# Expert loop of a two-block layer stack: GpSimd makes the low part of every fourth weight piece, and the loads wait for pieces to be used

## The chip, the cores and the metric

The kernel runs on one core of a Trainium2 chip. Its time is the device time of one execution in microseconds (us); lower is better. The engines are TensorE (PE; its weight loads are PEld), VectorE (DVE), ScalarE (ACT), GpSimd (POOL) and SyncE (SP), whose queue issues most of the loads from the chip's memory (HBM).

## What is computed

Two transformer-like blocks run one after the other on 256 tokens of width 1024, each with two layers. The change touches only the mixture of experts of the first block's second layer:

```python
def moe_ffn(h, router_w, w1, w3, w2):
    logits = (h @ router_w).astype(jnp.float32)
    top_vals, top_idx = lax.top_k(logits, TOP_K)            # 2 of 8 experts
    top_w = jax.nn.softmax(top_vals, axis=-1)
    gate = jnp.sum(jax.nn.one_hot(top_idx, N_EXPERTS, dtype=jnp.float32) * top_w[..., None], axis=-2)
    out = jnp.zeros_like(h)
    for e in range(N_EXPERTS):
        out = out + gate[..., e:e + 1].astype(h.dtype) * swiglu(h, w1[e], w3[e], w2[e])
    return out
```

`swiglu` is `(silu(h @ w1) * (h @ w3)) @ w2`, with `w1` and `w3` of 1024x2816 and `w2` of 2816x1024, all float32.

## The kernel before

**Passes.** After the router the kernel knows which tokens go to which expert. A pass is one expert with up to 128 of its tokens; the number of passes is read at run time, and the same loop body (`Fori`) runs on every engine. This input makes 8 passes.

**Steps and pieces.** Within a pass the hidden width of 2816 is cut into 11 chunks of 256, done in 12 steps, c = 0 to 11. Step c multiplies the tokens by chunk c of `w1` and `w3` (pieces q = 0 to 3, in steps 0 to 10) and the hidden values of chunk c-1 by its part of `w2` (pieces q = 4 and 5, in steps 1 to 11). A piece is 128 partitions by 1024 float32. A pass has 66 pieces (`ALL_PIECES`), numbered n in the order of PE's use: step 0 has n = 0 to 3, and step c has n = 6c-2+q.

**Split products.** To keep float32 precision each piece is split in two: ACT copies it to the rounded type fp32r (`w_hi`), and the low part is the piece minus `w_hi` (`w_lo`). PE then makes three products of 512 columns for each half of the piece: tokens' high part by `w_hi` (line 824), tokens' low part by `w_hi` (825), high part by `w_lo` (826), so 6 matmuls a piece. `w_hi` and `w_lo` have four places each (`NPIECE`), and piece n lies in place n % 4.

**Who waits for whom.** In the expert loop ACT (line 1551) makes `w_hi` of piece n when PE has used piece n-4 (semaphore `e_used`); DVE makes `w_lo` (its operation is recorded at the helper's line 2182) when `e_hi_ready` has counted piece n; PE waits for `e_split`, which DVE's low part raises. In other stages of the program GpSimd makes low parts too (line 700), by the same subtraction in the same shape.

**Other work of a step.** When q = 3 is used, ACT makes silu (L1569, output `xs`), DVE multiplies (L2346, `u_z`; one input in PSUM, the accumulators' memory), and PE turns the result by two transposes (L1106) at the start of the next step. ACT copies those out (`fhT_hi`, L1564), and DVE makes their low part (`fhT_lo`, L2182, one input in PSUM). DVE's order within a step is fhT_lo, low parts of q = 3, 4, 5 and of q = 0 of the next step, u_z, low parts of q = 1 and 2 of the next step. ACT's order is the same with high parts.

**Loads.** Weights land in three slots (`ring` 0 and 1, `third_gu`, each with a part of `down_w`); step c uses slot c % 3. SP issues the loads of step c (three of 1 MB; two in step 0, one in step 11) when all pieces of step c-3 are split (`e_split`, line 641). At the first step of the first pass the counts that open the loop come from two operations: DVE's copy of `slot_no` (line 2247) adds `ALL_PIECES` to `e_split`, and the fourth of PE's opening matmuls on `pb` (line 1084) adds `NPIECE` to `e_used`.

**Edges of a pass.** PE gathers the tokens of the next pass (L1093) and scatters the results (L1128); ACT and DVE copy the results out (L1571, L2353). Then ACT and DVE make the parts of pieces 0 to 2 and of the tokens (`hT_hi`, L1557, and `xg_lo`), and in the first steps DVE makes the selection tables (L2331 to L2335, L2297, L2298).

Of the kernel before, what the change touches and what calls it, by code (L numbers as in the profile page):

```python
# [15 lines left out]
F32 = mybir.dt.float32  # L16
# [3 lines left out]
ALU = mybir.AluOpType  # L20
# [14 lines left out]
NF = FF // FC  # L35
# [16 lines left out]
NSLOT = 3  # L52
# [183 lines left out]
def build(nc, a, out):  # L236
# [6 lines left out]
    with ctx:  # L243
# [176 lines left out]
            "sel_ready", "gather_mm", "xg_ready", "selT_ready", "scatter_mm", "ys_ready"))  # L420
        e_arrived = [sem(f"e_arrived{n}") for n in range(NSLOT)]
        e_silu, e_h, e_ht_mm, e_ht_hi, e_ht = (sem(s) for s in ("e_silu", "e_h", "e_ht_mm", "e_ht_hi", "e_ht"))
        zero_ready, moe_mm, sel_step = sem("zero_ready"), sem("moe_mm"), sem("sel_step")

        def step_loads(c):
# [181 lines left out]
        def expert_piece(c, q):  # L607
# [2 lines left out]
                return gu_slot(c % NSLOT)[:, q * PIECE:(q + 1) * PIECE]  # L610
            return down_w[:, c % NSLOT, (q - GU_PIECES) * PIECE:(q - GU_PIECES + 1) * PIECE]

        def slot_split(c):

            return pieces(c + 1) if c < NF else ALL_PIECES
# [17 lines left out]
        def expert_weights(sp):  # L633

            n_pass = passes(sp)
            with sp.Fori(0, n_pass) as t:
                e = sp.value_load(table[0:1, bass.ds(t, 1)], min_val=0, max_val=NE - 1)
                for c in range(NF + 1):
                    s = c % NSLOT

                    sp.wait_ge(e_split, t * ALL_PIECES + (ALL_PIECES + slot_split(c - NSLOT) if c >= NSLOT else slot_split(NF + 1 - NSLOT + c)))
                    srcs = []
                    if c < NF:
                        for view, w_ in ((gate_view, a["moe_w1"]), (up_view, a["moe_w3"])):
                            srcs.append((view, w_[0, bass.ds(e, 1), :, c * FC:(c + 1) * FC].rearrange("o (k p) n -> p (o k) n", p=P)))
                    if c:
                        srcs.append((down_view, a["moe_w2"][0, bass.ds(e, 1), (c - 1) * FC:c * FC, :].rearrange("o (k p) n -> p (o k) n", p=P)))
                    for view, src in srcs:
                        sp.dma_start(view(s, src), src).then_inc(e_arrived[s], 16)
            sp.wait_ge(e_split, n_pass * ALL_PIECES + ALL_PIECES)  # L650

# [41 lines left out]
        def _(pool):  # L695
# [47 lines left out]
            load_gain(5, a["g_pre_mix_2"][0])  # L743
            pool.wait_ge(gla_put, 10)
            pool.dma_start(cst2, cdram2[:, :]).then_inc(cst2_in, 16)
            for l in range(2):
                L, n = 2 + l, 5 + 4 * l
                if l:
                    load_gain(n, a["g_pre_mix_2"][l])
                low_parts(MIX[L], MIX[L] + 4)  # L750
                load_gain(n + 1, a["g_post_mix_2"][l])

                pool.wait_ge(merged_ready, 2 + l)
                for lo, w, name in ((0, MW, "g_cq_2"), (MW, P, "g_ckv_2"), (MW + P, MW, "g_sgu_v_2")):
                    pool.dma_start(ygain[:, lo:lo + w], a[name][l].partition_broadcast(P)).then_inc(ygain_in, 16)
                for aa in range(2):
                    for b_ in range(2):
                        pool.dma_start(pool_w[64 * b_:64 * b_ + 64, aa, :], a["pool_w_2"][l, 2 * aa + b_]).then_inc(pool_in_sem, 16)
                pool.wait_ge(filled, BK[L].filled(("turn", 3)))
                pool.dma_start(sgu_w, a["sgu_w_2"][l].rearrange("g i j -> i g j")).then_inc(sgu_in, 16)  # L760
                low_parts(MIX[L] + 4, MIX[L] + 40)
                pool.wait_ge(merged_ready, L + 1)
                load_gain(n + 2, a["g_pre_ffn_2"][l])
                load_gain(n + 3, a["g_post_ffn_2"][l])
                low_parts(MIX[L] + 40, MIX[L] + 44)
# [4 lines left out]
        def _(pe):  # L770
# [291 lines left out]
            def experts():  # L1062
# [20 lines left out]
                for n in range(4):  # L1083
                    ins = mm(pb[n][:], ident, scratch[:], start=True, stop=False, skip_group_check=True)
                    if n == 2:
                        ins.then_inc(scatter_mm, 1)
                    if n == 3:
                        ins.then_inc(e_used, NPIECE)

                def gather():  # L1090
                    for k in range(KD):
# [8 lines left out]
                with pe.Fori(0, n_pass) as t:  # L1100
                    pe.wait_ge(xg_ready, t + 1)
                    for n, (c, q) in enumerate(PIECE_LIST):
# [4 lines left out]
                            ins.then_inc(e_ht_mm, 1)  # L1107
                        if q == GU_PIECES:
                            pe.wait_ge(e_ht, t * NF + c)
                        pe.wait_ge(e_split, t * ALL_PIECES + ALL_PIECES + n + 1)  # L1110
                        if q < GU_PIECES:
                            for kk in range(2):
                                k = 2 * q + kk
# [230 lines left out]
        def _(act):  # L1344
# [195 lines left out]
            def experts():  # L1540
# [3 lines left out]
                with act.Fori(0, n_pass) as t:  # L1544
                    def high_parts(lo, hi):
                        for n in range(lo, hi):
                            c, q = PIECE_LIST[n]
                            if n == pieces(c):
                                act.wait_ge(e_arrived[c % NSLOT], e_landed(t, c))
                            act.wait_ge(e_used, t * ALL_PIECES + place_free(n) + NPIECE)  # L1550
                            f(w_hi[:, n % NPIECE], expert_piece(c, q), ACT.Copy).then_inc(e_hi_ready, 1)  # L1551

                    high_parts(0, 3)
# [5 lines left out]
                    for c in range(NF + 1):  # L1559
                        if c:  # L1560
                            high_parts(at, min(pieces(c) + 3, ALL_PIECES))
                            at = min(pieces(c) + 3, ALL_PIECES)
                            act.wait_ge(e_ht_mm, t * NF + c)
                            f(fhT_hi[:, :, 0:P], mb[3][:, 0:2 * P].rearrange("p (k s) -> p k s", k=2), ACT.Copy).then_inc(e_ht_hi, 1)  # L1564
                        if c < NF:
                            high_parts(at, pieces(c + 1) + 1)
                            at = pieces(c + 1) + 1
                            act.wait_ge(e_used, t * ALL_PIECES + pieces(c) + GU_PIECES + NPIECE)
                            f(fsg[:, 0, :], mb[2][:, 0:FC], ACT.Silu).then_inc(e_silu, 1)  # L1569
                    act.wait_ge(e_used, t * ALL_PIECES + ALL_PIECES + NPIECE)  # L1570
# [134 lines left out]
        def _(v):  # L1705
# [536 lines left out]
            def route():  # L2242
# [1 line left out]

                v.wait_ge(logits_mm, 1)
                link(cp(logit.rearrange("p t e -> p (t e)"), mb[0][:, 0:2 * NE]))
                cp(slot_no, const("iotap")).then_inc(e_split, ALL_PIECES)
                v.wait_ge(e_split, ALL_PIECES)
                rk = const("rank8").unsqueeze(1).to_broadcast([P, T, NE])
                wide = lambda col: col.unsqueeze(2).to_broadcast([P, T, NE])  # L2250
                for src, top, one in ((logit, m1, one1), (tmp16, m2, one2)):
# [51 lines left out]
            def experts():  # L2303
# [3 lines left out]
                with v.Fori(0, n_pass) as t:  # L2307
# [8 lines left out]
                    def low_parts(lo, hi):  # L2316
                        for m in range(lo, hi):
                            c, q = PIECE_LIST[m]
                            v.wait_ge(e_hi_ready, t * ALL_PIECES + m + 1)
                            low(w_lo[:, m % NPIECE], expert_piece(c, q), w_hi[:, m % NPIECE]).then_inc(e_split, 1)  # L2320

# [14 lines left out]
                    for c in range(NF + 1):  # L2336
# [10 lines left out]
                        if c == 0:  # L2347
# [1 line left out]
                            qv = quad[:, 0:2].rearrange("p q t -> p (q t)")  # L2349
                            step(ts(qv, qv, -float(P), None, ALU.add))  # L2350
                            select_places(step)
                    v.wait_ge(e_used, t * ALL_PIECES + ALL_PIECES + NPIECE)
                    cp(ys[:, 512:1024], mb[1][:]).then_inc(ys_ready, 1)  # L2353
                assert n[0] == 7, n[0]
                v.wait_ge(moe_mm, 1)
# [54 lines left out]
```

## Time and profile before

| | |
|---|---|
| three runs | 2878.45 us median, 2877.14 to 2897.91 |
| profiled execution | 2887.1 us, of which the profiled span is 2885.3 us |
| busy in the span: PE, DVE, ACT, POOL | 90%, 56%, 46%, 17% |
| low parts by POOL, whole program | 184, mean 2431 ns |
| low parts by DVE from `ring`, whole program | 352, mean 1223 ns |
| granted TensorE clock over the span | 0.94 of full speed |

Times in the rows below are microseconds from the start of the span. In a row of the timeline the first number is the start, the second the duration; "x2" merges two instructions of the same kind, whose durations then read as one stretch. Matmuls overlap: each shows some 0.4 us, but the next one of the same kind starts 0.23 us later. A bracket at the end tells how long the engine idled before, and what released it. SPq is the queue of SP that issues loads.

### The profile page before, as it was taken

How to read it: one execution, taken by the hardware profiler on the slowest of the kernel's cores; microseconds unless marked ns; L12 is line 12 of the kernel's file. 1: busy time of each engine (PE TensorE's matmuls, PEld its weight loads, DVE VectorE, ACT ScalarE, POOL GpSimd, SP SyncE). 2: the span in 40 equal slices, each digit the busy share in tenths (PEclk: the TensorE clock that was granted, in tenths of full speed). 3: DMA queues.
4: the chain of work that ended last, by engine and by line, in shares of the span. 5: the costliest groups of instructions: out<-in, count | busy, mean ns of one | idle time of the engine just before them, and what ended most of it. 6: DMA issues, size and time to landing. Idle time of an engine off the chain costs nothing.

```text
span 2885.3 us, 31104 instructions
## 1 busy us (share of the span) xinstructions
PE 2600.9 (90%) x11527; PEld 2049.5 (71%) x11527; DVE 1605.2 (56%) x2251; ACT 1319.5 (46%) x1687; POOL 477.1 (17%) x248
## 2 busy tenths in 40 slices
PE   6998789989987799999999999789979978998897
PEld 5886568868865677787787787577757856775786
DVE  2545545525365398898898898732325553231654
ACT  1333144413331277777787787524324432433443
POOL 2344210003442100000000000024430002444000
PEclk9989899999898799999999999999989998989999
DMA  5423175424231499999999899443355514334550
GB/s 183 161 103 123 44 242 175 152 76 161 102 131 58 141 360 307 321 340 318 322 325 334 305 340 333 176 151 117 131 181 184 182 68 131 137 109 168 191 197 35
DMA packets 373247, 549.38 MB, mean 190 GB/s; under 512 B 20828, under 2 KB 273104, under 8 KB 373024
## 3 DMA queue, kind: packets, MB, share of 16 engines
q1 hardware_dynamic: 369072, 535.82, 54.0%
q0 software_dynamic: 3648, 9.87, 1.2%
q10 hardware_dynamic: 432, 2.37, 0.2%
q8 instruction: 66, 1.08, 0.2%
q14 instruction: 29, 0.24, 0.0%
HBM read 546.98 MB, written 1.05 MB: 190 GB/s over the span
## 4 chain that ended last, share of the span: by engine, by line
PE 63%; DVE 8%; issue 2%; DMA 2%; ACT 2%; POOL 1%; SPq 0%; ACTq 0%; DVEq 0%
PE mb L824 12%; PE mb L826 11%; PE mb L825 11%; PE pb L824 5%; PE pb L825 5%; PE pb L826 5%; PE pb L802 3%; PE pb L1152 2%; PE pb L807 2%; DMA ring<-in_w_in 1%; DVE w_lo L2182 1%; POOL w_lo L700 1%; PE mb L1172 1%; PE pb L872 1%; PE mb L1174 1%
## 5 line engine op out<-in xcount | busy, mean ns | idle before, releaser
L700 POOL TENSOR_TENSOR w_lo<-ring,w_hi 128x1024 fp32r<-128x1024 f32 x184 | 443.4, 2431 | 1875.3 <-ACT w_hi L1418 1875.1
L824 PE MATMUL mb<-w_hi,hT_hi 128*128 128x512 f32 x1232 | 500.1, 406 | 24.3 <-DVE xg_lo L2182 9.7
L2182 DVE TENSOR_TENSOR w_lo<-ring,w_hi 128x1024 fp32r<-128x1024 f32 x352 | 423.6, 1223 | 121.3 <-ACT w_hi L1418 70.6
L826 PE MATMUL mb<-w_lo,hT_hi 128*128 128x512 f32 x1232 | 486.1, 395 | 0.0
L1418 ACT ACTIVATE w_hi<-ring 128x1024 fp32r<-128x1024 f32 x280 | 285.8, 1054 | 315.8 <-DMA ring<-in_w_in 153.9
L2182 DVE TENSOR_TENSOR w_lo<-down_w,w_hi 128x1024 fp32r<-128x1024 f32 x242 | 295.2, 1223 | 93.6 <-ACT w_hi L1418 79.3
L824 PE MATMUL pb<-w_hi,hT_hi 128*128 128x512 f32 x736 | 309.0, 420 | 16.9 <-DVE low_rows L2182 7.6
L825 PE MATMUL pb<-w_hi,low_rows 128*128 128x512 f32 x736 | 299.8, 407 | 0.0
L826 PE MATMUL pb<-w_lo,hT_hi 128*128 128x512 f32 x736 | 299.1, 406 | 0.0
L824 PEld LDWEIGHTS mb<-w_hi,hT_hi 128*128 128x128 f32 x1232 | 233.1, 189 | 80.5 <-issue 22.9
L1551 ACT ACTIVATE w_hi<-ring 128x1024 fp32r<-128x1024 f32 x256 | 268.1, 1056 | 42.6 <-PE mb L826 39.3
L825 PE MATMUL mb<-w_hi,xg_lo 128*128 128x512 f32 x704 | 276.1, 392 | 0.0
L826 PEld LDWEIGHTS mb<-w_lo,hT_hi 128*128 128x128 f32 x1232 | 232.4, 189 | 56.0
L825 PE MATMUL mb<-w_hi,low_rows 128*128 128x512 f32 x528 | 206.9, 392 | 0.0
L1551 ACT ACTIVATE w_hi<-down_w 128x1024 fp32r<-128x1024 f32 x176 | 187.2, 1063 | 37.4 <-PE mb L826 32.8
L824 PEld LDWEIGHTS pb<-w_hi,hT_hi 128*128 128x128 f32 x736 | 147.2, 200 | 54.7 <-DVE low_rows L2182 8.5
L2182 DVE TENSOR_TENSOR w_lo<-third_gu,w_hi 128x1024 fp32r<-128x1024 f32 x132 | 159.4, 1222 | 41.3 <-ACT w_hi L1418 31.6
L826 PEld LDWEIGHTS pb<-w_lo,hT_hi 128*128 128x128 f32 x736 | 146.1, 198 | 32.6
L825 PEld LDWEIGHTS pb<-w_hi,low_rows 128*128 128x128 f32 x736 | 147.0, 200 | 31.1 <-issue 1.3
L825 PEld LDWEIGHTS mb<-w_hi,xg_lo 128*128 128x128 f32 x704 | 133.4, 189 | 27.2
L802 PE MATMUL pb<-hT,ring 128*128 128x256 f32 (+1 forms) x608 | 137.2, 386 | 12.5 <-DMA ring<-in_w_in 11.3
L824 PE MATMUL mb<-w_hi,fhT_hi 128*128 128x512 f32 x352 | 140.0, 398 | 8.1 <-DVE fhT_lo L2182 8.1
(412 smaller groups left out, 3755.6 us busy)
## 6 DMA issues: line engine op xcount, KB each, us to landing
ring<-in_moe_w SPq DMA_DIRECT2D x128, 1024.0 KB, 7.7
ring<-in_w_in SPq DMA_DIRECT2D x48, 2048.0 KB, 7.7
down_w<-in_moe_w SPq DMA_DIRECT2D x88, 1024.0 KB, 10.9
third_gu<-in_moe_w SPq DMA_DIRECT2D x48, 1024.0 KB, 9.1
down_w<-in_w_ffn_down SPq DMA_DIRECT2D x22, 1024.0 KB, 9.8
ring<-in_w_out SPq DMA_DIRECT2D x8, 2048.0 KB, 7.9
ring<-in_ffn_w SPq DMA_DIRECT2D x16, 1024.0 KB, 7.9
ring<-in_w_ffn_gate SPq DMA_DIRECT2D x16, 1024.0 KB, 5.2
```

The costliest lines, as they stand in the source:

```text
L700: nc.gpsimd.tensor_tensor(w_lo[:, m % NPIECE], source[m][0], w_hi[:, m % NPIECE].bitcast(F32), ALU.subtract).then_inc(pool_split, 1)
L802: ins = mm(bank[0:m, n * S:(n + 1) * S], wv[:, k, col - chunk_lo:col - chunk_lo + m], hT[:, k, :], start=k == 0, stop=k == KD - 1)
L807: ins = mm(bank[:, 0:m], hT[:, k, i * P:(i + 1) * P], wv[:, k, col - chunk_lo:col - chunk_lo + m], start=k == 0, stop=k == KD - 1)
L824: mm(o, a_hi, hi, start=start, stop=False)
L825: mm(o, a_lo, hi, start=False, stop=False)
L826: return mm(o, a_hi, lo, start=False, stop=stop)
L872: ins = mm(bank[:], yT[:, b % 2, kk, i * P:(i + 1) * P], w[:, kk, h * 512:(h + 1) * 512], start=kk == 0, stop=kk == 1)
L1152: ins = mm(bank[:], src[:, kk, i * P:(i + 1) * P], w[:, kk, h * 512:(h + 1) * 512], start=kk == 0, stop=kk == n_k - 1)
L1172: ins = mm(o, qT[:, h, it], kT[:, h, jt], start=True, stop=i != j)
L1418: f(w_hi[:, m % NPIECE], src, ACT.Copy).then_inc(w_hi_ready, 1)
L1551: f(w_hi[:, n % NPIECE], expert_piece(c, q), ACT.Copy).then_inc(e_hi_ready, 1)
L2182: return tt(dst, src, hi.bitcast(F32), ALU.subtract)
```

## The change

In the expert loop the low part of every piece with n % 4 = 3 (n = 3, 7, ..., 63: 16 of the 66 pieces) is made by GpSimd in a loop of its own, and DVE leaves it out. PE waits for the new semaphore `e_pool_split` before those pieces and for `e_split` before the others. Since one count no longer tells that all pieces of a slot are split, SP waits for `e_used` before it loads a slot, and `e_used` now starts at `ALL_PIECES`.

```diff
+        POOL_PIECES = ALL_PIECES // NPIECE
+        DVE_PIECES = ALL_PIECES - POOL_PIECES
@@ SP, expert_weights
-                    sp.wait_ge(e_split, t * ALL_PIECES + (ALL_PIECES + slot_split(c - NSLOT) if c >= NSLOT else slot_split(NF + 1 - NSLOT + c)))
+                    sp.wait_ge(e_used, t * ALL_PIECES + (ALL_PIECES + slot_split(c - NSLOT) if c >= NSLOT else slot_split(NF + 1 - NSLOT + c)))
...
-            sp.wait_ge(e_split, n_pass * ALL_PIECES + ALL_PIECES)
+            sp.wait_ge(e_used, n_pass * ALL_PIECES + ALL_PIECES)
@@ GpSimd, before the second block's layers
+            nc.gpsimd.memset(small[:, 141:142], 0.0).then_inc(e_pool_split, POOL_PIECES)
+            n_pass = passes(pool)
+            with pool.Fori(0, n_pass) as t:
+                for m in range(NPIECE - 1, ALL_PIECES, NPIECE):
+                    pool.wait_ge(e_hi_ready, t * ALL_PIECES + m + 1)
+                    nc.gpsimd.tensor_tensor(w_lo[:, m % NPIECE], expert_piece(*PIECE_LIST[m]),
+                                            w_hi[:, m % NPIECE].bitcast(F32), ALU.subtract).then_inc(e_pool_split, 1)
@@ PE, experts
                     if n == 3:
-                        ins.then_inc(e_used, NPIECE)
+                        ins.then_inc(e_used, ALL_PIECES)
...
-                        pe.wait_ge(e_split, t * ALL_PIECES + ALL_PIECES + n + 1)
+                        if n % NPIECE == NPIECE - 1:
+                            pe.wait_ge(e_pool_split, t * POOL_PIECES + POOL_PIECES + n // NPIECE + 1)
+                        else:
+                            pe.wait_ge(e_split, t * DVE_PIECES + DVE_PIECES + n + 1 - n // NPIECE)
@@ ACT: the three waits on e_used have the new start
-                            act.wait_ge(e_used, t * ALL_PIECES + place_free(n) + NPIECE)
+                            act.wait_ge(e_used, t * ALL_PIECES + place_free(n) + ALL_PIECES)
@@ DVE, low_parts
                             c, q = PIECE_LIST[m]
+                            if m % NPIECE == NPIECE - 1:
+                                continue
```

**DVE, steps 2 and 3 of a pass.** The stretch runs from the low part of q = 3 of step 2 (`third_gu`) to the low part of q = 1 of step 3 (`ring`). Before:

```order
L2182 TENSOR_TENSOR w_lo<-third_gu,w_hi 128x1024
L2319 REGISTER_ALU
L2182 TENSOR_TENSOR w_lo<-down_w,w_hi 128x1024
L2319 REGISTER_ALU
L2182 TENSOR_TENSOR w_lo<-down_w,w_hi 128x1024
L2319 REGISTER_ALU
L2182 TENSOR_TENSOR w_lo<-ring,w_hi 128x1024
L2345 REGISTER_ALU
L2346 TENSOR_TENSOR u_z<-xs,mb 128x256
L2319 REGISTER_ALU
L2182 TENSOR_TENSOR w_lo<-ring,w_hi 128x1024
```

With the change (lines are 14 to 16 higher there):

```order
L2196 TENSOR_TENSOR w_lo<-third_gu,w_hi 128x1024
L2335 REGISTER_ALU
L2196 TENSOR_TENSOR w_lo<-down_w,w_hi 128x1024
L2335 REGISTER_ALU
L2196 TENSOR_TENSOR w_lo<-ring,w_hi 128x1024
L2361 REGISTER_ALU
L2362 TENSOR_TENSOR u_z<-xs,mb 128x256
L2335 REGISTER_ALU
L2196 TENSOR_TENSOR w_lo<-ring,w_hi 128x1024
```

One of the two low parts from `down_w` (n = 15, q = 5 of step 2) is gone from DVE's order; the rest stands as it stood.

**POOL, at the place between the two blocks.** Before, the load of constants is followed by the low parts of the second block:

```order
L745 DMA cst<-shape_constants 128x1856 [waits gla_put]
L700 TENSOR_TENSOR w_lo<-ring,w_hi 128x1024 [waits w_hi_ready] x4
L728 DMA gain<-in_g_post_mix 128x1024 [waits xn_ready]
```

With the change the loop stands between them; its first rows are these:

```order
L749 DMA cst<-shape_constants 128x1856 [waits gla_put]
L750 MEMSET small 128x1
L635 TENSOR_LOAD table [waits table_ready]
L635 ISA x2
L752 UNCONDITIONAL_BRANCH
L752 ISA
L755 TENSOR_TENSOR w_lo<-ring,w_hi 128x1024 [waits e_hi_ready]
L754 REGISTER_ALU
L755 TENSOR_TENSOR w_lo<-ring,w_hi 128x1024 [waits e_hi_ready]
L754 REGISTER_ALU
L755 TENSOR_TENSOR w_lo<-third_gu,w_hi 128x1024 [waits e_hi_ready]
```

These three are n = 3, 7 and 11. The pieces that went to POOL are, by step: q = 3 of step 0, q = 3 of every odd step to 9, and q = 1 and q = 5 of every even step from 2 to 10. No other work of POOL stands within the loop.

## Rows read from the trace of the kernel before

**Rows 1.** Waits in the expert loop, 990 to 1860 us: total, times, longest.

```profile
PE mb L824 <- DVE xg_lo L2182: 9.7, 8, 3.7
PE mb L824 <- DVE fhT_lo L2182: 8.1, 8, 1.0
PE mb L1106 <- DVE u_z L2346: 7.4, 8, 0.9
...
PE mb L824 <- DVE w_lo L2182: 6.3, 8, 0.8
```

**Rows 2.** Timeline of PE, second pass, steps 1 to 3.

```profile
1123.19 0.40 PE L824 MATMUL mb<-w_hi,hT_hi 128*128 128x512 f32 x1
...
1127.38 0.38 PE L1106 MATMUL mb<-cst,u_z 128*128 128x128 f32 x2
...
1134.59 0.40 PE L824 MATMUL mb<-w_hi,fhT_hi 128*128 128x512 f32 x1
...
1135.99 0.38 PE L1106 MATMUL mb<-cst,u_z 128*128 128x128 f32 x2
```

**Rows 3.** Timeline of ACT, the same steps.

```profile
1133.39 0.39 ACT L1569 ACTIVATE xs<-mb 128x256 f32<-128x256 f32 x1 [0.34 <-PE mb L826]
...
1136.69 1.05 ACT L1551 ACTIVATE w_hi<-ring 128x1024 fp32r<-128x1024 f32 x1
...
1140.60 1.06 ACT L1551 ACTIVATE w_hi<-ring 128x1024 fp32r<-128x1024 f32 x1 [0.33 <-PE mb L826]
```

**Rows 4.** Timeline of DVE, steps 1 to 2 of that pass.

```profile
1119.02 2.35 DVE L2182 TENSOR_TENSOR w_lo<-ring,w_hi 128x1024 fp32r<-128x1024 f32 x2
...
1125.03 1.21 DVE L2182 TENSOR_TENSOR w_lo<-third_gu,w_hi 128x1024 fp32r<-128x1024 f32 x1
1126.17 0.41 DVE L2346 TENSOR_TENSOR u_z<-xs,mb 128x256 f32<-128x256 f32 x1
1126.50 2.35 DVE L2182 TENSOR_TENSOR w_lo<-third_gu,w_hi 128x1024 fp32r<-128x1024 f32 x2
```

**Rows 5.** Timelines of 203 to 206 and 244 to 246.5 us, DVE and POOL.

```profile
203.73 1.95 DVE L1950 SCALAR_TENSOR_TENSOR probs<-probs,mb 128x384 f32<-128x384 f32 x4 [8.57 <-PE mb L879]
203.74 2.41 POOL L700 TENSOR_TENSOR w_lo<-ring,w_hi 128x1024 fp32r<-128x1024 f32 x1 [2.17 <-ACT w_hi L1418]
...
244.83 2.49 POOL L700 TENSOR_TENSOR w_lo<-ring,w_hi 128x1024 fp32r<-128x1024 f32 x1 [13.29 <-ACT w_hi L1418]
244.98 3.42 DVE L1851 TENSOR_TENSOR conv<-ch_in 128x1024 f32<-128x1024 f32 x1
```

**Rows 6.** The same, 246.5 to 251 us: both of POOL's instructions in one.

```profile
244.83 5.82 POOL L700 TENSOR_TENSOR w_lo<-ring,w_hi 128x1024 fp32r<-128x1024 f32 x2 [13.29 <-ACT w_hi L1418]
```

**Rows 7.** Timeline of ACT and POOL, one piece of a stage where POOL splits.

```profile
374.77 1.06 ACT L1418 ACTIVATE w_hi<-ring 128x1024 fp32r<-128x1024 f32 x1 [1.66 <-PE pb L826]
...
375.91 2.40 POOL L700 TENSOR_TENSOR w_lo<-ring,w_hi 128x1024 fp32r<-128x1024 f32 x1 [0.32 <-ACT w_hi L1418]
```

**Rows 8.** Timeline of SP's queue, the issue of step 6's loads.

```profile
1141.69 1.00 SPq L649 DMA_DIRECT2D ring<-in_moe_w  x2
1142.87 2.03 SPq L649 DMA_DIRECT2D down_w<-in_moe_w  x1
```

**Rows 9.** Load of `down_w` issued at 1176 to 1178 us: size, landing.

```profile
down_w<-in_moe_w SPq DMA_DIRECT2D x1, 1024.0 KB, 11.3
```

**Rows 10.** Timeline around the start of the loop, 972 to 1003 us.

```profile
986.18 5.49 SPq L649 DMA_DIRECT2D ring<-in_moe_w  x4
...
990.90 3.60 PE L1084 MATMUL pb<-scratch,cst 128*128 128x512 f32 x8
...
994.60 1.28 ACT L1551 ACT_TABLE_LOAD   x1 [14.49 <-DMA ring<-in_moe_w]
```

**Rows 11.** Timeline behind the loop, 1838 to 1905 us.

```profile
1846.82 3.73 PE L1093 MATMUL mb<-gates,xn 128*128 128x128 f32 x32
...
1868.38 3.88 ACT L1418 ACTIVATE w_hi<-ring 128x1024 fp32r<-128x1024 f32 x4
```

More of the change, by code:

```diff
@@ L422, in build @@
         e_silu, e_h, e_ht_mm, e_ht_hi, e_ht = (sem(s) for s in ("e_silu", "e_h", "e_ht_mm", "e_ht_hi", "e_ht"))
+        e_pool_split = sem("e_pool_split")
         zero_ready, moe_mm, sel_step = sem("zero_ready"), sem("moe_mm"), sem("sel_step")
@@ L1567, in experts @@
                             at = pieces(c + 1) + 1
-                            act.wait_ge(e_used, t * ALL_PIECES + pieces(c) + GU_PIECES + NPIECE)
+                            act.wait_ge(e_used, t * ALL_PIECES + pieces(c) + GU_PIECES + ALL_PIECES)
                             f(fsg[:, 0, :], mb[2][:, 0:FC], ACT.Silu).then_inc(e_silu, 1)
-                    act.wait_ge(e_used, t * ALL_PIECES + ALL_PIECES + NPIECE)
+                    act.wait_ge(e_used, t * ALL_PIECES + 2 * ALL_PIECES)
                     f(ys[:, 0:512], mb[0][:], ACT.Copy).then_inc(ys_ready, 1)
@@ L2246, in route @@
                 link(cp(logit.rearrange("p t e -> p (t e)"), mb[0][:, 0:2 * NE]))
-                cp(slot_no, const("iotap")).then_inc(e_split, ALL_PIECES)
-                v.wait_ge(e_split, ALL_PIECES)
+                cp(slot_no, const("iotap")).then_inc(e_split, DVE_PIECES)
+                v.wait_ge(e_split, DVE_PIECES)
                 rk = const("rank8").unsqueeze(1).to_broadcast([P, T, NE])
@@ L2351, in experts @@
                             select_places(step)
-                    v.wait_ge(e_used, t * ALL_PIECES + ALL_PIECES + NPIECE)
+                    v.wait_ge(e_used, t * ALL_PIECES + 2 * ALL_PIECES)
                     cp(ys[:, 512:1024], mb[1][:]).then_inc(ys_ready, 1)
```

## Prediction

> **What bounds the kernel now.** I read the waits of the expert loop first, since only this loop changes. PE is what the loop waits on: over eight passes it idles 9.7 + 8.1 + 7.4 + 6.3 = 31.5 us before its products, each eight times, so once a pass and at its edges [rows 1]. The timeline of PE then shows a step in the middle of a pass: from one pair of transposes to the next 1135.99 - 1127.38 = 8.61 us [rows 2]. Its 36 matmuls at 0.23 us fill that, so PE has no gap there. ACT and DVE run beside it: ACT makes the high part of q = 3 from 0.70 us after the transposes (1136.69) and that of the next q = 0 at 4.61 (1140.60), whenever PE has freed a place [rows 3]. DVE needs 1.21 us for a low part, takes up the next work 1.14 us after its start, and 0.33 us after u_z's [rows 4]. So in the middle of a pass a faster DVE brings nothing; the reader should ask what may make PE late.
>
> **The removed low parts.** DVE loses 16 of 66 low parts a pass. Where PE is gapless this is worth nothing. At the edges: `xg_lo` waits behind n = 0 to 2, which stay with DVE; `fhT_lo` of step 11 and `u_z` of step 0 wait for PE and ACT; the 6.3 us before a product with `w_lo` are n = 5, which starts at 1119.02 behind the selection work [rows 4] and stays with DVE. I take 0; the lower end is the whole of that wait, 6.3 us gained.
>
> **The added low parts.** POOL needs 2.40 us, and starts 0.08 us after ACT's end (374.77 + 1.06, then 375.91) [rows 7]. Alone that just fits: q = 3 of an odd step would be ready 0.70 + 1.06 + 0.08 + 2.40 = 4.24 us after the transposes. PE wants it at 4.41 (q = 5 starts at 1134.59, 7.21 after the transposes, less two pieces of 1.40) [rows 2, 3, 7]. The question is what both engines do at once. At 244.83 POOL makes a low part, and DVE's subtraction-like instruction of the same size, also with two inputs in SBUF, is handed out at 244.98 and takes 3.42 instead of 1.21 us: it ends at 248.40, 1.08 after POOL's first ends (247.32) [rows 5]. POOL's second then ends at 250.65, 2.25 after DVE's [rows 6]. So the two take turns, each a whole instruction, and a turn costs slightly less than the instruction alone. DVE's instructions with one input in PSUM don't take part: four at 203.73 take 1.95 in all beside POOL [rows 5]. All of DVE's low parts of weights have two inputs in SBUF; u_z and fhT_lo have one in PSUM.
>
> The Trainium skill, SBUF — State Buffer, section "Who interferes with whom", says that a VectorE instruction with two SBUF inputs and a GpSimd one that reads SBUF exclude each other for the whole of an instruction. The trace agrees that the later one waits; on the turn's length it shows 0.13 to 0.15 us less than whole instructions. By the page's rule taken literally the sum would be that of the second rival below.
>
> **The chain of turns.** From POOL's q = 3 of an odd step to its q = 5 of the next, an even one: DVE's q = 4, 5, 0 (1.08 + 1.14 + 1.14), POOL's q = 1 (2.25), DVE's q = 2 (1.08), fhT_lo (0.33), DVE's q = 3, 4 (2 x 1.14), POOL's q = 5 (2.25): 11.55 us. From there to the next odd q = 3: DVE's q = 0 (1.08), u_z (0.33), q = 1, 2 (2.28), POOL's q = 3 (2.25): 5.94. Together 17.49 us for two steps, for which PE needs 2 x 8.61 = 17.22. The other u_z and fhT_lo lie beside POOL. The chain hardly ever waits for ACT: it takes up q = 0 of the next step at 4.24 + 1.08 + 1.08 = 6.4 after the transposes, and ACT has it ready at 5.67 (1140.60 + 1.06) [rows 2, 3]. So the pair of engines, and no longer PE, sets the pace, by 0.27 us in two steps.
>
> Per pass it begins with n = 7. DVE is at n = 6 until 1119.02 + 2.35 = 1121.37, POOL's turn ends at 1123.62, and PE wanted n = 7 at 1123.19 [rows 2, 4]: 0.43 late. I add 0.20 for the signal and PE's new start, a choice. From n = 7 to n = 63 the chain takes 4 x 17.49 + 11.55 = 81.51 us. PE took 11.40 (1123.19 to 1134.59) + 8 x 8.61 = 80.28 [rows 2]: 1.23 more. Per pass 0.43 + 0.20 + 1.23 = 1.86, in eight passes **14.9 us**. n = 3 costs nothing: PE comes to it three pieces into the pass. The selection work that POOL's n = 3 may block (L2331 to L2335) is not waited for before the pass's end.
>
> **The wait for used pieces.** Three places. *First loads:* SP issues them at 986.18. ACT waits 14.49 us for them until 994.60, and all of the first pass's pieces follow from there. With the change SP waits for the count that PE's opening matmuls give, of which the fourth ends at 990.90 + 3.60 = 994.50 [rows 10]. So first load, first high part and PE's first product move by 994.50 - 986.18 = **8.3 us**, once. Nothing covers it; the bounds are 7.4 (the count may come with the start of the last matmul, 0.9 sooner) and 11 (PE idles longer before it and may be granted its lower clock for longer). *Middle of a pass:* a slot is reloaded now 5.70 us after the transposes (1141.69) [rows 8], behind the last low part; with the change at 7.21 + 1.40 + 0.2 = 8.8, so 3.1 later. The last of the three loads is issued 1.18 after the first and lands 11.3 us later even late in a pass [rows 8, 9]: at 8.8 + 1.2 + 11.3 = 21.3. ACT needs it at 2 x 8.61 + 4.61 = 21.8. Hidden, with 0.5 us to spare, and 0.3 more by the slower pace. *Behind the loop:* the next layer's loads start after the last use, some 5 us later, before 1847. They are needed at 1868.38 [rows 11], over 20 us later: nothing.
>
> **Sum.** 14.9 + 8.3 = 23.2 us. The profiled execution took 2887.1, so it would take 2910.3. The median of the runs shown lies 8.65 below it; I forecast 2878.45 + 23.2 = **2901.7**, so 2902 us (+0.8%).
>
> **Rivals.**
> 1. *Forecast* (45%): turns as above, 2902; by itself 2893 to 2914, from 7.4 at the start and 1 us a pass, to 11 and 3 us.
> 2. *Whole turns* (25%): no overlap at the hand-over. Two steps then take 3 x 2.40 + 3 x 1.21 + 6 x 1.14 + 2 x 0.33 = 18.33, the half up to q = 5 12.11, and the chain 85.43, 5.15 over PE. n = 7 is 0.58 + 0.20 late. 8 x 5.93 + 8.3 = 55.7: 2934. For it: the overlap rests on two hand-overs in one place, and any slower signal from POOL adds to it. Against it: those rows [rows 5, 6].
> 3. *Loads come late* (12%): if they land more than 0.5 us later than now, each chain of issue, landing and use, three steps long, grows by the rest. At 1.5 us later this is 3 x 1.0 x 8 = 24 more: 2926. For it: 0.5 us is little. Against it: at the slower pace less traffic queues up.
> 4. *No turns* (13%): the instructions run side by side in this loop; then only the start costs: 2878.45 + 8.3 = 2887. Against it: the 3.42 us for a 1.21 us instruction [rows 5].
> 5. *Faster* (5%): DVE without n = 3 reaches n = 5 sooner, and the first loads aren't on the path. It decides if n = 5 starts 0.8 us sooner; then 6.3 us are gained: 2872. Against it: before n = 5 DVE waits for silu and selects, whatever it did before [rows 4], and ACT did wait for the first load [rows 10]. Over 1% faster would take more than 28.8 of the 31.5 us of waits [rows 1].
>
> **Numbers.** What a measurement of this kernel can tell from no change is about 1%, 28.8 us: the bounds are 2849.7 and 2907.2. Slower by over 1% are rival 2 (0.25), most of 3 (0.10) and the upper quarter of 1 (0.12): 0.47. Faster by over 1%: 0.02. Within 1%: 0.51. Range 2886 to 2936: from rival 4 to just over rival 2.
>
> **What would show it.** Right: DVE low parts of 2.3 to 3.5 us beside POOL's instructions, POOL's of up to 3.4; PE gaps of 0.1 to 0.6 us before n = 7 of each pass, before q = 5 of even and q = 3 of odd steps; a step of 8.7 to 8.8 us in the mean, a pass 1.9 us longer than before; first expert load issued near 994.5; no wait of ACT for a load but the first. Wrong: DVE's at 1.22 throughout (rival 4); two steps at 18.3 (rival 2); ACT waiting for loads in the middle of a pass (rival 3); the first load still at 986 (start term).

## The result and the profile after

| | before | after | difference |
|---|---|---|---|
| device time, median of 4 runs each | 2881.31 us (2877.14 to 2897.91) | 2920.77 us (2910.86 to 2922.43) | ratio 1.012 (95%: 1.008 to 1.0159) |
| device time, second comparison, 24 and 6 runs | 2881.26 us | 2907.26 us | ratio 1.0088 (1.0069 to 1.0106) |
| profiled execution, span | 2885.3 us | 2920.6 us | +35.3 us |
| busy: PE, DVE, ACT, POOL | 90%, 56%, 46%, 17% | 90%, 55%, 45%, 28% | |
| granted TensorE clock over the span | 0.94 | 0.939 | |

The kernel became slower by about 1%. The two comparisons give +39.5 and +26.0 us between medians, against +23.2 forecast; the time of 2920.8 lies in the range given (2886 to 2936), 19.1 us above the 2901.7 forecast.

The first question is where the 35.3 us of the profiled span are. The windows view cuts both traces at the same three instructions: POOL's load of the final norm's gain, PE's first product of the expert loop, and the load of `merged` for the next layer. Columns: window, its length, busy time of PE, PEld, DVE, ACT and POOL with counts of instructions, granted clock, share of the DMA engines, GB/s. Before:

```profile
0.00:965.58 965.58, 845.33 (x3862) 675.94 (x3863) 452.29 (x738) 300.84 (x393) 253.22 (x135) 0.92 0.37 128
965.58:1001.81 36.23, 23.49 (x115) 20.82 (x114) 15.26 (x55) 10.02 (x13) 1.61 (x3) 0.64 0.58 197
1001.81:1881.90 880.09, 827.82 (x3672) 652.62 (x3672) 740.04 (x827) 639.34 (x749) 12.40 (x11) 0.98 0.92 314
1881.90:2885.30 1003.40, 904.29 (x3880) 700.16 (x3880) 397.59 (x632) 369.26 (x532) 209.88 (x102) 0.93 0.42 142
```

After:

```profile
0.00:971.29 971.29, 850.13 (x3862) 679.00 (x3863) 452.61 (x738) 300.72 (x393) 253.46 (x135) 0.92 0.37 127
971.29:1014.23 42.94, 21.68 (x115) 18.76 (x114) 15.27 (x55) 10.02 (x13) 2.71 (x5) 0.66 0.49 164
1014.23:1911.21 896.98, 841.35 (x3672) 644.22 (x3672) 752.08 (x699) 639.16 (x749) 352.81 (x138) 0.99 0.91 308
1911.21:2920.60 1009.39, 909.03 (x3880) 702.91 (x3880) 397.88 (x632) 369.44 (x532) 209.52 (x102) 0.93 0.42 141
```

The expert loop (third row) is 16.9 us longer, the start of the loop (second row) 6.7. The other 11.7 us stand in the first row (+5.7) and the last (+6.0), where both kernels execute the same 3862 and 3880 matmuls and the change touches nothing. A second trace of the changed kernel, cut in the same way, has +2.0, +8.3, +16.5 and -4.3 us in the four rows. So the loop's part repeats (16.9 and 16.5). The start's is 6.7 and 8.3: the 115 matmuls of that row kept PE busy for 21.68 us at a granted clock of 0.66 in the first trace, and for 23.39 at 0.61 in the second. What stands outside does not repeat. Over ten traces (this kernel's two, that of before, and those of the experiments but 6) the first row runs from 959.15 to 971.29 us and the last from 993.49 to 1009.39, and the first trace of the changed kernel has the longest of both. The granted clock of the last row is 0.93 in the three traces where it is longest (1003.40, 1006.10, 1009.39) and 0.94 in the seven others.

Now the loop, by its waits from 990 to 1900 us (total, times, longest). They answer to [rows 1]:

```profile
PEld mb L835 <- POOL w_lo L755: 30.2, 80, 0.8
...
ACT L1565 <- DMA ring<-in_moe_w: 23.4, 1, 23.4
...
PE mb L835 <- DVE xg_lo L2196: 18.3, 8, 12.3
...
PE mb L835 <- DVE fhT_lo L2196: 8.6, 8, 1.1
PE mb L1117 <- DVE u_z L2362: 7.4, 8, 0.9
PE mb L835 <- DVE w_lo L2196: 6.4, 8, 0.8
...
PE mb L835 <- POOL w_lo L755: 2.7, 8, 0.3
...
ACT w_hi L1565 <- DMA down_w<-in_moe_w: 0.4, 1, 0.4
```

The waits at a pass's edges are what they were: `fhT_lo` 8.6 (was 8.1), `u_z` 7.4 (7.4), `w_lo` 6.4 (6.3). Only the first wait for `xg_lo` grew, from 3.7 to 12.3. New are the waits for POOL: ten times a pass TensorE's weight load sits before a low part of POOL, and once a pass PE itself does, for 0.3 us. (Such a wait partly overlaps matmuls still running, so 30.2 is not PE's loss.) ACT waited for a load once more only, for 0.4 us.

How the turns run is best seen in two steps of the second pass. POOL's timeline (start, duration, instruction; the bracket is the idle time ahead and what ended it):

```profile
1134.35 3.30 POOL L755 TENSOR_TENSOR w_lo<-ring,w_hi 128x1024 fp32r<-128x1024 f32 x1 [8.06 <-ACT w_hi L1565]
...
1146.37 2.87 POOL L755 TENSOR_TENSOR w_lo<-down_w,w_hi 128x1024 fp32r<-128x1024 f32 x1 [3.09 <-ACT w_hi L1565]
1152.62 2.58 POOL L755 TENSOR_TENSOR w_lo<-ring,w_hi 128x1024 fp32r<-128x1024 f32 x1 [3.38 <-ACT w_hi L1565]
...
1163.89 2.90 POOL L755 TENSOR_TENSOR w_lo<-down_w,w_hi 128x1024 fp32r<-128x1024 f32 x1 [3.06 <-ACT w_hi L1565]
```

DVE's timeline beside them:

```profile
1145.75 1.22 DVE L2196 TENSOR_TENSOR w_lo<-down_w,w_hi 128x1024 fp32r<-128x1024 f32 x1
1147.72 2.60 DVE L2196 TENSOR_TENSOR w_lo<-ring,w_hi 128x1024 fp32r<-128x1024 f32 x1 [0.75 <-ACT w_hi L1565]
1150.24 0.41 DVE L2362 TENSOR_TENSOR u_z<-xs,mb 128x256 f32<-128x256 f32 x1
1150.57 2.35 DVE L2196 TENSOR_TENSOR w_lo<-ring,w_hi 128x1024 fp32r<-128x1024 f32 x2
```

Read them as ends. DVE's `down_w` piece ends at 1146.97, POOL's at 1149.24, 2.27 us later. DVE's next one, handed out at 1147.72, ends at 1150.32: 1.08 after POOL's. It shows 2.60 us for work of 1.21. DVE's two ring pieces end at 1152.92, POOL's next at 1155.20, 2.28 later. `u_z` at 1150.24 takes its usual 0.41. Each low part of one engine stands in the way of the other's, as in [rows 5, 6].

PE's timeline of the same stretch gives the pace, by the pairs of transposes, and the late n = 7:

```profile
1136.50 0.40 PE L835 MATMUL mb<-w_hi,hT_hi 128*128 128x512 f32 x1
...
1137.70 0.50 PE L835 MATMUL mb<-w_hi,hT_hi 128*128 128x512 f32 x1 [0.34 <-POOL w_lo L755]
...
1150.79 0.38 PE L1117 MATMUL mb<-cst,u_z 128*128 128x128 f32 x2
...
1159.54 0.38 PE L1117 MATMUL mb<-cst,u_z 128*128 128x128 f32 x2
...
1168.35 0.38 PE L1117 MATMUL mb<-cst,u_z 128*128 128x128 f32 x2
```

Two steps take 1168.35 - 1150.79 = 17.56 us, where they took 2 x 8.61 = 17.22 [rows 2].

### The profile page after: what moved, and what is told of

Read it like the earlier page. It is cut to its first block, busy times and chain, and to the rows that moved or that the text cites. A ratio compares the mean times of both kernels' runs of the same rounds, so it can differ in the third digit from the quotient of the medians.

```text
span 2920.6 us, 31125 instructions
## 1 busy us (share of the span) xinstructions
PE 2622.2 (90%) x11527; PEld 2044.9 (70%) x11527; DVE 1617.8 (55%) x2123; ACT 1319.3 (45%) x1687; POOL 818.5 (28%) x377
## 3 DMA queue, kind: packets, MB, share of 16 engines
q10 hardware_dynamic: 432, 2.37, 0.2%
q8 instruction: 66, 1.08, 0.2%
## 4 chain that ended last, share of the span: by engine, by line
PE 40%; issue 19%; POOL 11%; DVE 7%; DMA 2%; ACT 2%; POOLq 0%; DVEq 0%; ACTq 0%
POOL w_lo L755 10%; PE pb L835 5%; PE pb L836 5%; PE pb L837 5%; PE mb L835 4%; PE mb L837 4%; PE mb L836 4%; PE pb L813 3%; PE pb L1166 2%; PE pb L818 2%; DMA ring<-in_w_in 1%; POOL w_lo L704 1%; PE mb L1186 1%; PE pb L883 1%; PE mb L1188 1%
## 5 line engine op out<-in xcount | busy, mean ns | idle before, releaser
L704 POOL TENSOR_TENSOR w_lo<-ring,w_hi 128x1024 fp32r<-128x1024 f32 x184 | 443.2, 2430 | 1013.9 <-ACT w_hi L1432 1013.7
L2196 DVE TENSOR_TENSOR w_lo<-ring,w_hi 128x1024 fp32r<-128x1024 f32 x288 | 409.4, 1438 | 132.2 <-ACT w_hi L1432 70.6
L2196 DVE TENSOR_TENSOR w_lo<-down_w,w_hi 128x1024 fp32r<-128x1024 f32 x202 | 312.5, 1563 | 99.7 <-ACT w_hi L1432 79.1
L755 POOL TENSOR_TENSOR w_lo<-ring,w_hi 128x1024 fp32r<-128x1024 f32 x64 | 166.1, 2595 | 354.9 <-ACT w_hi L1565 354.9
```

Of the source, the lines that this page charges most:

```text
L704: nc.gpsimd.tensor_tensor(w_lo[:, m % NPIECE], source[m][0], w_hi[:, m % NPIECE].bitcast(F32), ALU.subtract).then_inc(pool_split, 1)
L755: nc.gpsimd.tensor_tensor(w_lo[:, m % NPIECE], expert_piece(*PIECE_LIST[m]), w_hi[:, m % NPIECE].bitcast(F32), ALU.subtract).then_inc(e_po ...
L2196: return tt(dst, src, hi.bitcast(F32), ALU.subtract)
```

## The experiments

"After" below is the changed kernel. The length of the loop is given as the time from its first product to the first load of the layer behind it, which in the changed kernel waits for the last use of a piece. The start is the time from POOL's load of the final norm's gain to the first product. All of it is read from timelines. The start holds some microseconds that vary ahead of the first load; from the first load to the first product it is 15.5 to 15.8 us in all kernels but 6 (16.7) and 8 (15.1).

| kernel | ratio to before (95%) | start | loop |
|---|---|---|---|
| before | 1 | 36.23 | (840.75, its load waits for the split) |
| 1 only the wait for used pieces | 1.0046 (1.0032 to 1.006) | 44.58 | 844.32 |
| 2 after, with an early count | 1.0058 (1.0036 to 1.0079) | 36.16 | 862.41 |
| 3 as 2, DVE with a PSUM input | 1.0007 (0.999 to 1.0024) | 36.29 | 845.03 |
| 4 after, once more | 1.0088 (1.0069 to 1.0106) | 44.54 | 861.72 |
| 5 as 2, DVE compares in SBUF | one run, 2887.90 us | 36.23 | 862.24 |
| 6 as 2, POOL every second piece | one run, 3011.72 us | 37.31 | 975.48 |
| 7 as 2, POOL every twelfth piece | 0.999 (0.9966 to 1.0015) | 34.12 | 844.00 |
| 8 POOL only n = 2, selection at the end | 0.9962 (0.9942 to 0.9981) | 35.74 | 832.84 |
| 9 before, selection at the end | 0.9992 (0.997 to 1.0013) | 36.41 | (833.66, its load waits for the split) |

**1. Only the wait for used pieces.** DVE makes all low parts, as before.

```diff
-                    sp.wait_ge(e_split, t * ALL_PIECES + (ALL_PIECES + slot_split(c - NSLOT) ...
+                    sp.wait_ge(e_used, t * ALL_PIECES + (ALL_PIECES + slot_split(c - NSLOT) ...
...
-                        ins.then_inc(e_used, NPIECE)
+                        ins.then_inc(e_used, ALL_PIECES)
```

> The kernel before with only the SP waits changed: a slot is loaded again when its pieces are used, and the opening count of used pieces (66) comes from the fourth of PE's opening matmuls, as in the change; DVE makes all low parts. Theory (loads later only cost at the start): first expert load some 8.5 to 9 us later, passes as before at 106.3 us, the whole 9 us slower (+0.3%). Rival (late loads cost in every pass): ACT waits for loads in the middle of passes and a pass is longer by 0.5 us or more, in all 13 us or more.

Measured: 2893.63 us (12 runs) against 2881.26. The timeline at the start shows the first load and ACT's wait for it:

```profile
995.62 5.44 SPq L649 DMA_DIRECT2D ring<-in_moe_w  x4
...
1004.01 1.28 ACT L1551 ACT_TABLE_LOAD   x1 [22.69 <-DMA ring<-in_moe_w]
```

ACT waits 22.69 us instead of 14.49 [rows 10], and the start is 44.58 - 36.23 = 8.35 us longer. In the loop all waits are those of before, and no load is waited for but the first. From the first product to the load of `merged`, the window used above, it is 879.21 us against 880.09. So the wait costs its start term and nothing in the passes. The timed difference (9.2 to 17.3 us by the interval) is a little more than 8.35. The median granted clock of these 12 runs is 0.940, that of the 24 runs of before 0.944; how much time went with that in the runs of before stands below, under the sum, and it is more than the rest.

**2. The changed kernel with an early count.** A small memset of DVE gives the opening count, so that PE's opening matmuls no longer hold the first loads.

```diff
@@ PE
-                    if n == 3:
-                        ins.then_inc(e_used, ALL_PIECES)
@@ DVE, behind its copy of the logits
+                nc.vector.memset(small[:, 142:143], 0.0).then_inc(e_used, ALL_PIECES)
```

> The changed kernel, but the opening count of used pieces is given by DVE right behind its copy of the router's logits, where the opening count of split pieces was given before. GpSimd makes every fourth low part, and the loads still wait for used pieces. Theory (turns plus start): the first load is 0.2 us or less behind the table as before the change, a pass stays at 108.5 us; the whole is 9 us faster than the changed kernel and 17 us slower than the kernel before (+0.6%). Rival (the start costs nothing because something else holds the first pass): as slow as the changed kernel.

Measured: 2897.67 us (7 runs). The first load is issued at 986.24, as before the change, and the loop's waits are these:

```profile
PEld mb L835 <- POOL w_lo L755: 30.1, 80, 0.8
...
PE mb L835 <- DVE xg_lo L2194: 9.6, 8, 3.7
```

The start term is gone (36.16 us, and `xg_lo` back at 9.6), and the waits for POOL stay. Its loop is 862.41 - 844.32 = 18.1 us longer than that of experiment 1. This is GpSimd's part of the change, apart from the start.

**3. DVE with one input in PSUM.** As 2, but from piece 4 on DVE compares `w_hi` with an accumulator bank in PSUM (`pb`) instead of subtracting it from the piece. Those low parts are thereby left out. The instruction has the same size and the same place in DVE's order.

```diff
+                            if m >= NPIECE:
+                                two = lambda a_: a_.rearrange("p (h n) -> p h n", h=2)
+                                tt(two(w_lo[:, m % NPIECE]), pb[0][:].unsqueeze(1).to_broadcast([P, 2, 512]),
+                                   two(w_hi[:, m % NPIECE]).bitcast(F32), ALU.is_equal).then_inc(e_split, 1)
+                                continue
```

> As e2, but from piece 4 of each pass on DVE's instruction for its own pieces compares w_hi with an accumulator bank in PSUM instead of subtracting w_hi from the weights: same length, one input in SBUF instead of two. This leaves the low parts of those pieces out of the result. GpSimd's instructions stay as they are. Theory (the two engines take turns for instructions with two SBUF inputs): DVE's stay near 1.22 us and GpSimd's near 2.4 us throughout, no wait of PE for GpSimd beyond 0.1 us, a pass is back at 106.3 us within 0.3. Rival (GpSimd is too slow or its signal too late by itself, whatever DVE does): PE still waits some 0.4 us for GpSimd about ten times a pass, and a pass stays at 108 us or more.

Measured: 2884.64 us (10 runs). The instructions of DVE's line and of POOL's line, durations in ns as least, median, longest:

```profile
L2337 DVE TENSOR_TENSOR w_lo<-pb,w_hi x376: 1214/1225/1227, 1006.6 to 1841.9; 128x1024 fp32r<-128x1024 f32 x188
```

```profile
L755 POOL TENSOR_TENSOR w_lo<-ring,w_hi x64: 2357/2413/2427, 1001.6 to 1833.3; 128x1024 fp32r<-128x1024 f32 x64
L755 POOL TENSOR_TENSOR w_lo<-down_w,w_hi x40: 2414/2420/2422, 1026.2 to 1838.8; 128x1024 fp32r<-128x1024 f32 x40
```

And its waits from 990 to 1900 us:

```profile
ACT w_hi L1563 <- DMA down_w<-in_moe_w: 4.4, 8, 0.8
...
PEld mb L835 <- POOL w_lo L755: 2.9, 18, 0.2
```

With its second SBUF input gone DVE never takes longer than 1.227 us, POOL never longer than 2.429 (its pieces from `third_gu`), and PE hardly waits for POOL: 2.9 us instead of 30.1. The loop is back within 0.7 us of experiment 1. So POOL's 2.4 us by themselves cost next to nothing; the turns do.

The Trainium skill, SBUF — State Buffer, section "Who interferes with whom", says that a VectorE instruction with at most one SBUF input, outside the two-port modes, does not contend with GpSimd. This trace agrees, by the 1225 ns.

In this run loads are just late: ACT waits for `down_w` once a pass, up to 0.8 us. It cost PE nothing that can be seen.

**4. The changed kernel once more**, unedited.

> The changed kernel once more, on the same chip and in the same rounds as the others. Theory: outside the expert loop it does what the kernel before does, so a second trace shows other differences outside the loop than the 9.5 us of the first one, and the loop again 25 to 26 us longer. Rival (the change costs something behind the loop as well): again 6 us more between the end of the loop and the end of the program.

Measured: 2907.26 us (6 runs), 26.0 us over before. Start 44.54 - 36.23 = 8.3, loop 861.72 - 844.32 = 17.4 over experiment 1: 25.7 together. Behind the loop its trace is 4.3 us shorter than that of before, so the change costs nothing there.

**5. The control for 3.** The same comparison with both inputs in SBUF, in one run. Low parts are left out in this one too.

```diff
+                            if m >= NPIECE:
+                                tt(w_lo[:, m % NPIECE], expert_piece(c, q), w_hi[:, m % NPIECE].bitcast(F32),
+                                   ALU.is_equal).then_inc(e_split, 1)
+                                continue
```

> The control for e3: DVE makes the same comparison from piece 4 on, but with the weights in SBUF as its other input, so two inputs in SBUF; the low parts are left out in the same way. Turns: DVE's instructions beside GpSimd's take 2.3 to 3.5 us again and a pass takes 108.4 us, as in the changed kernel. Rival (in e3 it was the comparison and not the place of the input that made room): a pass of 106.3 us as in e3.

Measured, by the same view of both lines:

```profile
L2336 DVE TENSOR_TENSOR w_lo<-ring,w_hi x168: 1207/1214/2646, 999.4 to 1846.9; 128x1024 fp32r<-128x1024 f32 x168
L2336 DVE TENSOR_TENSOR w_lo<-down_w,w_hi x136: 1208/1214/3102, 1008.7 to 1852.9; 128x1024 fp32r<-128x1024 f32 x136
```

```profile
L755 POOL TENSOR_TENSOR w_lo<-ring,w_hi x64: 2354/2514/3310, 994.4 to 1843.1; 128x1024 fp32r<-128x1024 f32 x64
L755 POOL TENSOR_TENSOR w_lo<-down_w,w_hi x40: 2863/2893/2919, 1019.3 to 1848.6; 128x1024 fp32r<-128x1024 f32 x40
```

The waits for POOL are back (30.3 us, 80 times), and so is the loop (862.24). What counts in experiment 3 is where the input lies, not the operation. The time of this one run is only 1.5 us over the median of before because other stretches were short: POOL's load of the gain comes at 959.15 us instead of 965.58, and from the load of `merged` to the end it takes 993.60 us instead of 1003.40. Its loop is read from the trace, and no timed difference rests on the run.

**6. POOL makes every second piece.**

```diff
-        POOL_PIECES = ALL_PIECES // NPIECE
+        by_pool = lambda m: m % 2 == 1
+        POOL_PIECES = sum(by_pool(m) for m in range(ALL_PIECES))
```

> As e2, but GpSimd makes every second low part (odd n) instead of every fourth. Turns, each of 2.28 us on GpSimd and 1.08 on DVE: a pair of steps takes at least 6 x 2.28 + 6 x 1.08 = 20.2 us instead of 17.5, so a pass some 14 to 20 us longer than 108.5, the whole over 110 us slower than before. Rival (no turns, GpSimd only late by its own length): GpSimd alone needs 6 x 2.4 = 14.4 us in two steps, less than PE's 17.2; a pass stays at 107 to 109 us.

Measured: 3011.72 us in one run, beside a median of 2886.4 for before. Its waits:

```profile
PEld mb L837 <- POOL w_lo L757: 144.1, 211, 1.6
...
PE mb L837 <- POOL w_lo L757: 48.0, 144, 1.2
```

The loop is 975.48 - 844.32 = 131 us longer, 16.4 a pass. If each piece costs the pair its turn, a pass of 66 pieces should take about 33 x 2.28 + 33 x 1.1 = 112 us of turns, plus u_z, fhT_lo and the edges, against 106.3 of before. The pass came to 106.3 + 16.4 = 122.7. In the middle of the second pass PE's pairs of transposes start at 1168.22, 1178.27 and 1188.32 us: 20.10 for two steps, where six turns of each engine make 6 x (2.28 + 1.08) = 20.16. So the bound by turns holds, and twice as many pieces cost seven times as much, because at a quarter the chain is only 0.34 us over PE's 17.22 in two steps, and at a half 2.88.

**7. POOL makes n = 11, 23, 35, 47 and 59 only** (the same edit with `m % 12 == 11`).

> As e2, but GpSimd makes only every twelfth low part (n = 11, 23, 35, 47, 59: q = 1 of even steps), the one that comes in time in the changed kernel's trace. Turns: one turn of 2.28 us and eleven low parts of DVE (1.08 + 10 x 1.14 + 3 x 0.33) make 15.8 us in two steps, less than PE's 17.2, and this turn starts with a free port: no wait of PE for GpSimd, a pass of 106.3 us, the whole within 0.2% of before. Rival (any work of GpSimd beside DVE costs): a pass over 106.8 us.

Measured: 2877.13 us (10 runs) against 2886.4, ratio 0.999 (0.9966 to 1.0015). PE waits for no low part of POOL, and the loop (844.00) is that of experiment 1. Sparse turns are hidden, and DVE's freed time still brings nothing.

**8. Only n = 2 for POOL, and the selection moved from the first step of a pass to the last.** This edit goes for the waits at the edges that neither kernel had touched: `xg_lo` stands behind n = 0 to 2, and n = 5 behind the selection [rows 1, 4].

```diff
+        by_pool = lambda m: m == 2
...
-                        if c == 0:
+                        if c == NF:
                             v.wait_ge(sel_ready, t + 1)
```

> A version meant to beat both, from where PE does wait: the opening count early as in e2, GpSimd makes only n = 2 of each pass, so that DVE comes to xg_lo one low part sooner, and DVE's selection work moves from step 0 to the end of the pass, where DVE waits anyway, so that n = 5 is no longer behind it. Theory: 0.8 us a pass before n = 5 and up to 0.6 us before n = 0 are gained, a pass of 104.9 to 105.5 us, the whole 6 to 11 us faster than before (0.2 to 0.4%). Rival (the waits only move to the next instruction): a pass of 106.3 us, no change.

Measured: 2875.53 us (12 runs) against 2886.4: faster than the kernel before by 0.38% (0.19 to 0.58), and so than the changed one, which the second comparison has 0.9% over before. Its waits:

```profile
PE mb L837 <- DVE xg_lo L2196: 5.6, 8, 3.3
...
PEld mb L837 <- DVE w_lo L2196: 2.7, 8, 0.3
```

PE's wait for `xg_lo` falls from 9.7 to 5.6 us, that for `w_lo` (6.3) is gone, and the loop is 11.5 us shorter than in experiment 1.

**9. The selection alone**, moved in the kernel before.

```diff
-                        if c == 0:
+                        if c == NF:
```

> The kernel before with one edit of e8 alone: DVE's selection work (five instructions) moves from step 0 of a pass to its end; DVE makes all low parts and the loads wait for split pieces. Theory (both edits of e8 are worth what they take from PE's waits): the wait before n = 5 goes from 6.3 us to 0.5 or less in all, 0.7 to 0.8 us a pass, 6 us in all (0.2%); the wait behind xg_lo stays at 9.7 us. Rival (the selection then holds up the gather at the end of a pass): the wait moves to the gather, no gain in all.

Measured: 2881.04 us (10 runs) against 2884.36, a difference that the interval does not settle. The trace does:

```profile
PE mb L824 <- DVE xg_lo L2182: 9.9, 8, 3.9
...
PEld mb L824 <- DVE w_lo L2182: 2.7, 8, 0.4
```

PE's wait for `w_lo` is gone, that for `xg_lo` is not, and the loop is 840.75 - 833.66 = 7.1 us shorter. So of the 11.5 us of experiment 8 the selection brings 7.1. That leaves 4.4 for n = 2 on POOL, which was not run alone; 4.1 of them are what PE's wait for `xg_lo` lost, since DVE has one piece less ahead of it.

## Why the prediction was right

**What bounds the kernel.** Right. Removing low parts from DVE brought nothing where PE is gapless: in experiment 7 the loop is 0.3 us shorter, in experiment 3 PE runs at the pace of before.

**The turns.** Right, in kind and nearly in size. POOL's turn behind DVE was taken as 2.25 us and is 2.27 to 2.28; DVE's behind POOL 1.08, as taken. The half up to POOL's q = 5 came to 1166.79 - 1155.20 = 11.59 us (forecast 11.55), the other half to 1155.20 - 1149.24 = 5.96 (5.94). Two steps: 17.56 against 17.49 forecast and 17.22 of PE. Experiments 3 and 5 show that these turns are the cause: they come and go with DVE's second SBUF input.

**The sizes per pass.** POOL's n = 7 ends at 1137.65, and PE starts at 1137.70 where its work (1136.50 + 0.70) would have let it start at 1137.20: 0.50 late, forecast 0.43 + 0.20. From there to POOL's end of n = 63 it is 81.78 us; PE took 80.28 before, so 1.50 more instead of 1.23. That is the mis-sized term: three turns of POOL in two steps, each 0.02 to 0.03 longer than taken. Together 2.00 a pass against 1.86. The pass itself shows a little more, by POOL's n = 3 in two passes:

```profile
1123.92 2.37 POOL L755 TENSOR_TENSOR w_lo<-ring,w_hi 128x1024 fp32r<-128x1024 f32 x1 [12.96 <-ACT w_hi L1565]
```

```profile
1232.39 2.38 POOL L755 TENSOR_TENSOR w_lo<-ring,w_hi 128x1024 fp32r<-128x1024 f32 x1 [12.97 <-ACT w_hi L1565]
```

These lie 108.47 us apart. Before, PE's products of n = 5 behind their wait lay 1226.58 - 1120.29 = 106.29 apart, so a pass is 2.18 longer. Over eight passes the loop grew by 17.4 to 18.1 us against experiment 1, forecast 14.9. The 0.18 a pass that the two terms leave lies in the last steps of the pass, by PE's timeline. From the first product of n = 63 to the transposes behind it are 1.51 us (1219.48 to 1220.99), where before they were 1.39 (1203.45 to 1204.84): after its wait PE's second product starts 0.34 us behind the first, instead of 0.23. And the next product, which waits for `fhT_lo`, starts 1.45 us after the transposes, where before it was 1.39. That is 0.12 + 0.06 = 0.18; the prediction had neither term, small as they are.

**The start.** Right. Forecast 8.3, measured 8.35 in experiment 1 and 8.3 in 4. In the first trace of the changed kernel its rows are these:

```profile
994.39 4.00 PE L1095 MATMUL pb<-scratch,cst 128*128 128x512 f32 x8
...
998.57 5.53 SPq L653 DMA_DIRECT2D ring<-in_moe_w  x4
...
1007.01 1.28 ACT L1565 ACT_TABLE_LOAD   x1 [23.44 <-DMA ring<-in_moe_w]
```

SP issues the first load 0.2 us after PE's opening matmuls end (998.39). Experiment 2 takes this away.

**Loads in the middle of a pass, and behind the loop.** Right in its outcome, too kind in its margin. The load was forecast 8.8 us after the transposes of its step. It is issued at 1151.12, 9.12 after those at 1142.00, in the changed kernel, and 8.91 after them in experiment 3. The margin was worked out as 0.5 us at PE's pace and 0.3 more at the slower one. With the change ACT waited once, 0.4 us. At the full pace (experiment 3) it waited once a pass, up to 0.8 us: the 0.5 us were not there. In experiments 1, 7 and 8, at the full pace too, no such wait shows, so the margin is some tenths around zero, and which way it falls was not explained. Behind the loop nothing showed.

**The rivals.** Whole turns (2934 us) asked for a chain of 85.43 us from n = 7 to n = 63; it is 81.78. Late loads asked for waits of ACT in every pass. No turns (2887) would have DVE at 1.22 us throughout. Faster asked for n = 5 sooner; its wait is 6.4 us (6.3 before), and n = 5 is not reached sooner, since DVE waits for silu and selects first, as the prediction said. Its way to a gain was real all the same: experiments 8 and 9 get it, by moving what stands ahead of n = 5.

**The sum.** Forecast +23.2; start and loop together are 6.7 + 16.9 = 23.6 us in the first trace and 8.3 + 16.5 = 24.8 in the second, against before. That the first comes so close is partly luck: its loop is 2.0 us over the forecast and its start 1.6 under. The second comparison of medians is +26.0, the first +39.5. The surplus of the first is not in the change's places: of the profiled 35.3 us, 11.7 lie where both kernels do the same. The forecast was 19.1 us under the first median: 2.9 of that is the median of before, which came out as 2881.31 instead of 2878.45, and 16.3 is 39.5 less 23.2. The step that was off is thus the last one, from the sum to a median of four runs, which I forecast with no term for how such a median varies. The record does show what went with the surplus. The mean granted clock of the four runs was 0.939, 0.941, 0.937 and 0.938; that of the six runs of the second comparison, of the same kernel, 0.940 to 0.945, and these were 13.5 us faster in the median. In the 24 runs of before the time falls as the clock rises, from 2887.33 and 2889.63 us at 0.940 to 2871.33 and 2872.60 at 0.948: some 2 us for each 0.001, by my estimate from these. At equal clocks the two kernels lie about 26 us apart: 2914.98 against 2887.33 and 2889.63 at 0.940, 2906.25 and 2908.26 against 2876.96 to 2885.22 at 0.944. So most of the surplus went with a lower granted clock; what lowered it in those four runs is open, and no run here sets the clock by itself.

That the change makes the kernel slower is shown by both intervals; whether by more than 1% (1.012, then 1.0088) they leave open, as the nearly even chances did.

## What to carry to other kernels

Before work is handed from VectorE to GpSimd, count what both read. Where both read SBUF and VectorE's had two inputs there, as here, the second engine added no throughput: add up the turns (here 2.28 and 1.1 us) over a period, and compare with the pace of the engine that bounds. Giving GpSimd work was free while that sum stayed under the pace (5 pieces of 66). Above it the bill rises fast: 16 pieces cost 2.2 us a pass, and 17 more another 14.2, some 0.8 us each.

If VectorE isn't the bound, look where the bounding engine waits at the edges and change what stands ahead there: moving a few small instructions out of the way brought 7.1 us, while 128 large ones (16 in each of 8 passes) taken from VectorE brought nothing.

When the condition of a load is moved to another semaphore, ask who gives its opening count: here it was given 8.3 us later, on the path.

## What the runs showed of the hardware

A small instruction of VectorE waited for a whole one of GpSimd, and not only with two tensor inputs. In experiment 6, POOL's timeline (two low parts in one row) and DVE's at the same time:

```profile
1505.40 4.79 POOL L757 TENSOR_TENSOR w_lo<-ring,w_hi 128x1024 fp32r<-128x1024 f32 x2 [6.41 <-ACT w_hi L1565]
```

```profile
1504.95 0.29 DVE L2312 TENSOR_SCALAR gates<-cst,gates 128x128 f32<-128x128 f32 x1
1505.27 0.35 DVE L2313 SCALAR_TENSOR_TENSOR gates<-cst,gates 128x128 f32<-128x128 f32 x1
1505.66 2.29 DVE L2312 TENSOR_SCALAR gates<-cst,gates 128x128 f32<-128x128 f32 x1
1507.98 2.37 DVE L2313 SCALAR_TENSOR_TENSOR gates<-cst,gates 128x128 f32<-128x128 f32 x1
```

The tensor_scalar, which reads one tensor and one column of scalars, takes 2.29 us where the same instruction takes 0.29 before POOL starts, and the one behind it 2.37 instead of 0.35: each ends just behind one low part of POOL.

The Trainium skill, SBUF — State Buffer, section "Who interferes with whom", names `tensor_scalar` among the instructions that can take the shared ports. The trace agrees that it had to wait, by the 2.29 us; in which mode it ran no row shows.

The same stretch of a program, with the same 3880 matmuls, took from 993.49 to 1009.39 us in ten traces, the granted clock being 0.93 in the three longest and 0.94 in the others. A difference of 10 us between two single executions of this kernel says nothing of a change, unless the clocks are compared too.
